# w_o with the samples' two parts in one stationary block, and VectorE's residual taken in halves

## The chip, the core and the metric

The kernel runs on one core of a Trainium2 chip. A time is the device time of one execution in microseconds (us); beside it the hardware profiler gives a trace of one execution, with its span. The engines are TensorE (PE in the rows; PEld is its loading of stationary weights), VectorE (DVE), ScalarE (ACT), GpSimd (POOL) and SyncE (SP), which issues most of the transfers. Each works through a queue of its own in order and waits for the others on semaphores.

## What is computed

One layer of a decoder trunk, for 512 rows of a prompt and 8 rows of samples that share the weights. After the mixer's branches are merged into m, the output projection w_o, a gated residual, a second norm and the router follow, and then the experts that the router chose:

```python
def _mixer(h, buf_a, buf_b, buf_c, pos0, w_in, conf_dw, conf_dw_b, conf_ln_g, conf_ln_b,
           conf_pw, pool_w, pool_scale, sc_dw, sc_out, w_o):
    ...
    m = jax.nn.sigmoid(z_ga) * y_a + jax.nn.sigmoid(z_gb) * y_b + jax.nn.sigmoid(z_gc) * y_c
    return jnp.einsum('btd,de->bte', m, w_o), nb_a, nb_b, nb_c

def _moe(h, rg, rg_b, re, re_b, w1, w3, w2):
    ...
    gp = jax.nn.softmax((hf @ rg + rg_b).astype(jnp.float32), axis=-1)
    gidx = jnp.argmax(gp, axis=-1)
    ...
    el = (hf @ re + re_b).astype(jnp.float32).reshape(-1, N_GROUPS, EXP_PER_GROUP)
    ...
    for e in range(N_EXPERTS):
        act = jax.nn.silu(hf @ w1[e]) * (hf @ w3[e])
        y = y + (act @ w2[e]) * comb[:, e:e + 1]
    return y.reshape(b, t, d)

def _run_group(x, c, st_a, st_b, st_c, pos0, P):
    ...
        sh1, s1, g1, sh2, s2, g2 = jnp.split(mod[:, None, :], 6, axis=-1)
        h = _rmsnorm(x, P['norm1_g'][l]) * (1 + s1) + sh1
        m, na, nb, nc = _mixer(h, ...)
        x = x + g1 * m
        h = _rmsnorm(x, P['norm2_g'][l]) * (1 + s2) + sh2
        x = x + g2 * _moe(h, P['router_g'][l], P['router_g_b'][l], P['router_e'][l], ...)
    y = _rmsnorm(x, P['final_g'])
```

D_MODEL is 1024, there are 4 groups of 4 experts with 512 hidden columns each.

## The kernel before

The 520 rows are five row tiles: four of 128 prompt rows, and tile 4 with the 8 samples. All large products keep float32 accuracy by splitting both operands into two parts (hi and lo, type fp32r) and adding three products: hi x hi, hi x lo, lo x hi (`three`, L652 to L659). Weights arrive by SP's queue in quarters of 128x1024 into a ring of 6 raw slots; ScalarE makes the hi part of a quarter (`hi`, L1148), VectorE the lo part (`lo`, L1592), into rings of 4 slots; TensorE's semaphore quarter_used frees a slot. The order on each engine is written out by hand.

The stage of this change runs from 417 to 506 us of the trace:

- w_o has 1024 output columns, taken as two passes of 512. Its stationary operand is a block of the merged rows (hT_hi, hT_lo: 128 channels x the rows of a tile), its moving operand 512 columns of w_o. The first pass (L897 to L907) goes through the 8 blocks of channels, and in each through the five tiles, three matmuls each, into PSUM banks 0 to 4. The second pass (`w_o_tile`) goes tile by tile, 24 matmuls each, into banks 5 and 6 in turn; tile i waits for t_ready i-1, so that VectorE has read tile i-2's bank.
- Behind each tile VectorE does `residual` (x1 += gate x result: two multiplies of 512 columns and one add of 1024), `row_means`, and for the tile before it `second_norm`: four tiny operations for the reciprocal root, then h2 = x1 x r x scale and h2 += shift, 1024 columns each.
- ScalarE squares and sums each tile of x1 (`squares_of`), copies the transposed h2 of tile i-2 out of PSUM (`turned_h2`), issues the store of h2 of tile i-1 (`store_h2`) and takes the root (`root_of`), in this order for i = 0 to 6; at i = 5 it first splits two quarters of expert weights (`his(0, 2)`).
- TensorE puts between the tiles of the second pass the transposes of h2 (`router_turn`) and the router's logits (`router_logits`), and fills in "gap products": 16 products of 512 columns (L953) for a gate that is needed only at the end, 2, 2, 4, 1, 6 and 1 of them in six places. Their weights are loaded by `gap_load` on SP's queue; gap_prepared says that their 16-column stationary operand c_pad and the scales are ready.

```python
            for i in range(NTILE + 2):
                if i < NTILE:
                    w_o_tile(i)
                ...
                if i >= 3:
                    router_logits(i - 3)
                if i >= 2:
                    router_turn(i - 2)
            router_logits(NTILE - 1)
```

From the last logits VectorE works out each row's experts (L1982 to L2000), TensorE counts them, and the first 128 rows for the experts are gathered; the experts' loop runs on to the end.

## Time and profile before

| | |
|---|---|
| median of 3 runs | 871.22 us (870.71 to 872.97) |
| the profiled execution | 873.34 us, its span 871.5 us |
| TensorE busy | 837.3 us, 96% of the span |
| VectorE busy | 686.0 us, 79% |
| ScalarE busy | 465.5 us, 53% |
| GpSimd busy | 77.0 us, 9% |

The span is what the trace covers; 1.84 us of the execution lie around it. A row of a timeline gives the start, the duration, engine and line, what is written and read, and in brackets how long the engine was idle before and what ended that. A matmul's duration covers its way through the pipeline, so the distance from start to start is what one costs in a stream. An fp32 matmul stands as two entries.

### The profile page before, as it was taken

What the parts mean: (1) busy time and instruction counts of PE and PEld (TensorE: products, weight loads), DVE (VectorE), ACT (ScalarE), POOL (GpSimd) and SP (SyncE); (2) the same over time, 40 slices, a digit from 0 to 9 for tenths busy, and PEclk for the clock granted to TensorE, in tenths of its full rate; (3) what the DMA queues carried; (4) which work ended last, traced back from release to release, by engine and by line L of the source; (5) the groups of instructions that cost most, each with busy time, mean ns of one, the idle gap of its engine ahead of it and who ended that gap; (6) DMA issues with size and microseconds to landing.
All of it is one profiled execution on the core that took longest, in us unless ns stands there. A gap on an engine that the chain in (4) does not pass through costs nothing.

```text
span 871.5 us, 14885 instructions
## 1 busy us (share of the span) xinstructions
PE 837.3 (96%) x5035; PEld 699.3 (80%) x5035; DVE 686.0 (79%) x942; ACT 465.5 (53%) x556; POOL 77.0 (9%) x71
## 2 busy tenths in 40 slices
PE   7899999999999999999999889999999999999994
PEld 2589999989899999899777457888888888887851
DVE  0681638878798679599438879999989999899888
ACT  4552442343422221642222457888888888888852
POOL 0002000000000000230000001000100001003750
PEclk9889999999999999999999999999999999999998
DMA  9858545445443321123671579988896899999962
GB/s 329 276 166 277 200 126 170 138 151 164 148 152 118 97 80 66 55 74 123 237 251 73 175 275 390 393 313 317 312 400 219 322 398 400 400 399 397 359 196 98
DMA packets 90997, 201.24 MB, mean 231 GB/s; under 512 B 8792, under 2 KB 13400, under 8 KB 90918
## 3 DMA queue, kind: packets, MB, share of 16 engines
q1 hardware_dynamic: 78813, 165.25, 53.8%
q0 software_dynamic: 5136, 18.42, 6.0%
q10 hardware_dynamic: 7003, 16.95, 5.2%
q8 instruction: 30, 0.49, 0.2%
q14 instruction: 15, 0.12, 0.0%
HBM read 182.97 MB, written 18.35 MB: 231 GB/s over the span
## 4 chain that ended last, share of the span: by engine, by line
PE 81%; DVE 9%; DMA 3%; ACT 2%; issue 2%; SPq 1%; ACTq 1%; POOL 0%; POOLq 0%; DVEq 0%
PE ps L806 31%; PE ps L657 12%; PE ps L659 12%; PE ps L658 12%; PE ps L886 3%; DVE w_lo L1592 2%; PE ps L1001 2%; DMA region_a<-in_x_prompt_dram 2%; PE ps L1123 1%; PE ps L685 1%; PE ps L686 1%; PE ps L838 1%; ACT w_hi L1148 1%; DMA region_b<-h_rows,slot_idx 1%; PE ps L1036 1%
## 5 line engine op out<-in xcount | busy, mean ns | idle before, releaser
L1592 DVE TENSOR_TENSOR w_lo<-raw,w_hi 128x1024 fp32r<-128x1024 f32 x202 | 241.5, 1225 | 100.1 <-ACT w_hi L1148 98.3
L1148 ACT ACTIVATE w_hi<-raw 128x1024 fp32r<-128x1024 f32 x202 | 207.9, 1056 | 198.2 <-PE ps L806 150.6
L657 PE MATMUL ps<-w_hi,hT_hi 128*128 128x512 f32 (+1 forms) x512 | 205.6, 401 | 3.6 <-DVE w_lo L1592 1.4
L659 PE MATMUL ps<-w_hi,hT_lo 128*128 128x512 f32 (+1 forms) x512 | 202.1, 395 | 0.0
L658 PE MATMUL ps<-w_lo,hT_hi 128*128 128x512 f32 (+1 forms) x512 | 201.5, 393 | 0.0
L806 PE MATMUL ps<-hT_hi,w_hi 128*128 128x260 f32 x768 | 156.4, 285 | 1.9 <-ACT region_b L1242 1.1
L806 PE MATMUL ps<-hT_lo,w_hi 128*128 128x260 f32 x768 | 155.0, 283 | 0.0
L806 PE MATMUL ps<-hT_hi,w_lo 128*128 128x260 f32 x768 | 154.9, 283 | 0.0
L806 PEld LDWEIGHTS ps<-hT_hi,w_hi 128*128 128x128 f32 x768 | 118.8, 189 | 5.2 <-DVE w_lo L1592 3.9
L806 PEld LDWEIGHTS ps<-hT_lo,w_hi 128*128 128x128 f32 x768 | 119.4, 190 | 0.0
L806 PEld LDWEIGHTS ps<-hT_hi,w_lo 128*128 128x128 f32 x768 | 118.9, 189 | 0.0
L657 PEld LDWEIGHTS ps<-w_hi,hT_hi 128*128 128x128 f32 (+1 forms) x512 | 94.6, 185 | 28.8 <-DVE w_lo L1592 3.1
L1592 DVE TENSOR_TENSOR w_lo<-region_a,w_hi 128x1024 fp32r<-128x1024 f32 x90 | 110.3, 1244 | 6.2 <-ACT w_hi L1148 5.6
L659 PEld LDWEIGHTS ps<-w_hi,hT_lo 128*128 128x128 f32 (+1 forms) x512 | 94.5, 184 | 24.2
L658 PEld LDWEIGHTS ps<-w_lo,hT_hi 128*128 128x128 f32 (+1 forms) x512 | 94.7, 185 | 22.5
L1148 ACT ACTIVATE w_hi<-region_a 128x1024 fp32r<-128x1024 f32 x90 | 95.2, 1062 | 28.1 <-PE ps L659 28.1
L1739 DVE SCALAR_TENSOR_TENSOR region_b<-region_b,pT 128x512 f32<-128x512 f32 x120 | 81.7, 735 | 0.0
L1518 POOL DMA_INDIRECT region_b<-h_rows,slot_idx x18 | 23.0, 1280 | 381.0 <-DVE slot_idx L1969 271.4
L1592 DVE TENSOR_TENSOR hT_lo<-ps,hT_hi 128x512 fp32r<-128x512 f32 (+1 forms) x37 | 34.4, 933 | 13.0 <-ACT hT_hi L1401 10.4
L1497 POOL TENSOR_TENSOR hT_lo<-region_b,hT_hi 128x520 fp32r<-128x520 f32 x8 | 12.0, 1531 | 297.1 <-ACT hT_hi L1263 275.6
L1255 ACT ACTIVATE region_a<-ps 128x520 f32<-128x520 f32 x24 | 14.6, 606 | 33.7 <-PE ps L806 33.7
L685 PE MATMUL ps<-w_hi,cT 128*48 128x512 f32 x64 | 27.1, 423 | 2.0 <-DVE w_lo L1592 1.7
(337 smaller groups left out, 838.6 us busy)
## 6 DMA issues: line engine op xcount, KB each, us to landing
raw<-in_exp_w_dram SPq DMA_DIRECT2D x96, 512.0 KB
region_a<-in_exp_w_dram SPq DMA_DIRECT2D x80, 512.0 KB
raw<-in_w_in_dram SPq DMA_DIRECT2D x48, 512.0 KB
raw<-in_w_ada_dram SPq DMA_DIRECT2D x30, 512.0 KB
expert_rows<-region_b ACTq DMA_DIRECT2D x17, 512.0 KB, 6.3
region_b<-in_exp_w_dram SPq DMA_DIRECT2D x16, 512.0 KB
region_b<-in_w_ada_dram SPq DMA_DIRECT2D x14, 512.0 KB, 8.1
expert_rows<-region_a POOLq DMA_DIRECT2D x8, 512.0 KB, 8.4
```

The source lines that it names most:

```text
L657: pe.matmul(out, pairs[0], moving[0], start=start, stop=False)
L658: pe.matmul(out, pairs[0], moving[1], start=False, stop=False)
L659: return pe.matmul(out, pairs[1], moving[0], start=False, stop=stop)
L685: pe.matmul(ps[0:C_LO + 16, bank, :], cT[:, kk, :], hi[:, k, :], start=(kk == 0), stop=False)
L806: mm = pe.matmul(ps[:, 2 * m + h, 0:HT], w[:, k, ms], x[:, kk, h * HT:(h + 1) * HT], start=start, stop=stop)
L886: mm = pe.matmul(ps[:, 2 * s + h, 0:HT], w[:, k, (t % 2) * P:(t % 2 + 1) * P], x[:, kk, h * HT:(h + 1) * HT], start=start, stop=stop)
L1001: t = pe.transpose(ps[:, 2 + k // 4, (k % 4) * P:(k % 4 + 1) * P], xg[:, k * P:(k + 1) * P], ident[:, :])
L1148: act.activation(w_hi[:, split_slot(n), :], place, ACT.Copy).then_inc(hi_done, 1)
L1255: act.activation(split(gates[:, 4 * (g - 6) + m, :]), halves(m), ACT.Sigmoid).then_inc(set_free[m], 1)
L1518: pool.indirect_dma_start(xg, None, h2_dram, bass.IndirectOffsetOnAxis(ap=slot_idx[:, :], axis=0)).then_inc(xg_ready, 16)
L1592: return dve.tensor_tensor(out, whole, first.bitcast(F32), ALU.subtract)
L1739: dve.scalar_tensor_tensor(va[:, c, 0:NP], ua[:, c, t:t + NP], w, va[:, c, 0:NP], ALU.mult, ALU.add).then_inc(conv_step, 1)
```

## The change

- A tile cT of 48 columns for each of the 8 channel blocks exists before (it holds the conditioning for the adaLN products, hi part in columns 0 to 15 and lo part from column C_LO = 32). When those products are over, VectorE forms c_pad from it early (gap_prepared 1), and GpSimd copies the samples' hi and lo parts of the merged rows into columns 0 to 7 and 32 to 39, block by block behind VectorE's lo part (sampled_ready).
- w_o's tile 4 then takes this block of 40 columns as stationary operand, with two matmuls (w_o's hi, w_o's lo) in place of three; the two parts' results stand in PSUM rows 0 to 7 and 32 to 39 and are added by VectorE.
- VectorE's residual is cut into a left half (columns 0 to 511, out of the first pass' banks) and a right half. The left halves of tiles 0 and 1 stand behind the first pass, those of 2, 3 and 4 between the steps of tiles 0 and 1. `second_norm` of a tile now follows in the tile's own turn; the scale is multiplied in ahead of the root (`scaled`), and the root and the shift go in one operation.
- The scaling of SC2 moves ahead of the last two lo parts of w_o; SP's fourth gap_load waits for gap_prepared 2, which comes with it. The gap products stand 1, 1, 5, 1, 6 and 2 in the six places.

ScalarE's and SP's order is the same as before. The first place is VectorE ahead of w_o's second pass. Before, all four lo parts (L1592, the first of them stands above the piece), the scales, c_pad, and the first tile's residual:

```order
L1592 TENSOR_TENSOR w_lo<-raw,w_hi 128x1024 [waits hi_done] x3
L1895 SCALAR_TENSOR_TENSOR region_a<-region_a 128x1024 [waits ld_dec,ld_bcast]
L1896 SCALAR_TENSOR_TENSOR region_a<-region_a 8x1024 [waits dve_step]
L1897 TENSOR_TENSOR small<-cT 128x128 [waits gap_prepared]
L1930 TENSOR_TENSOR region_b<-ps,region_a 128x512 [waits ld_router,wo_done,ld_x,gap_prepared]
```

The same place in the changed kernel, with its own line numbers (L1609 is the lo part, L1953 and L1954 are a left half, L1969 and L1970 a right half, L1979 is `scaled`):

```order
L1609 TENSOR_TENSOR w_lo<-raw,w_hi 128x1024 [waits hi_done,dve_step]
L1609 TENSOR_TENSOR w_lo<-raw,w_hi 128x1024 [waits hi_done]
L1913 SCALAR_TENSOR_TENSOR region_a<-region_a 128x1024 [waits ld_dec,ld_bcast]
L1914 SCALAR_TENSOR_TENSOR region_a<-region_a 8x1024 [waits dve_step]
L1609 TENSOR_TENSOR w_lo<-raw,w_hi 128x1024 [waits hi_done,gap_prepared]
L1609 TENSOR_TENSOR w_lo<-raw,w_hi 128x1024 [waits hi_done]
L1953 TENSOR_TENSOR region_b<-ps,region_a 128x512 [waits quarter_used,ld_router,ld_x]
L1954 TENSOR_TENSOR region_a<-region_a,region_b 128x512 [waits dve_step]
L1953 TENSOR_TENSOR region_b<-ps,region_a 128x512 [waits dve_step]
L1954 TENSOR_TENSOR region_a<-region_a,region_b 128x512 [waits dve_step]
L1969 TENSOR_TENSOR region_b<-ps,region_a 128x512 [waits wo_done,dve_step]
```

The scales moved ahead of two lo parts, c_pad is gone from here, and two left halves stand ahead of the first wait for w_o's second pass.

The second place is VectorE around the samples' residual. Before, from the residual of tile 3 on (L1914 to L1918 are the root of tile 2, L1942 and L1944 its h2, L1908 and L1924 the mean of tile 3 and a logit tile):

```order
L1930 TENSOR_TENSOR region_b<-ps,region_a 128x512 [waits wo_done,ms_ready]
L1931 TENSOR_TENSOR region_b<-ps,region_a 128x512
L1932 TENSOR_TENSOR region_a<-region_a,region_b 128x1024 [waits t_ready]
L1914 RECIPROCAL sums<-sums 128x1 [waits root_ready,x1_ready]
L1916 SCALAR_TENSOR_TENSOR sums<-sums 128x1 [waits dve_step]
L1917 TENSOR_SCALAR sums<-sums 128x1 [waits dve_step]
L1918 TENSOR_TENSOR sums<-sums 128x1 [waits dve_step]
L1942 SCALAR_TENSOR_TENSOR region_b<-region_a,sums 128x1024 [waits dve_step]
L1944 TENSOR_TENSOR region_b<-region_b,region_a 128x1024 [waits dve_step]
L1908 TENSOR_SCALAR sums<-sums 128x1 [waits ssq_ready]
L1924 TENSOR_TENSOR region_b<-ps,rbias 128x20 [waits logit_done,ms_ready]
L1930 TENSOR_TENSOR region_b<-ps,region_b 8x512 [waits quarter_used]
```

After, the same stretch; L1933 to L1937 are now the root of tile 3 itself, L1985 its h2:

```order
L1969 TENSOR_TENSOR region_b<-ps,region_a 128x512 [waits wo_done]
L1970 TENSOR_TENSOR region_a<-region_a,region_b 128x512 [waits t_ready]
L1979 TENSOR_TENSOR region_b<-region_a 128x1024 [waits h2_stored0,h2T_done,x1_ready]
L1927 TENSOR_SCALAR sums<-sums 128x1 [waits ssq_ready,dve_step]
L1943 TENSOR_TENSOR region_b<-ps,rbias 128x20 [waits logit_done,ms_ready]
L1933 RECIPROCAL sums<-sums 128x1 [waits root_ready]
L1935 SCALAR_TENSOR_TENSOR sums<-sums 128x1 [waits dve_step]
L1936 TENSOR_SCALAR sums<-sums 128x1 [waits dve_step]
L1937 TENSOR_TENSOR sums<-sums 128x1 [waits dve_step]
L1985 SCALAR_TENSOR_TENSOR region_b<-region_b,sums,region_a 128x1024 [waits dve_step]
L1967 TENSOR_TENSOR region_b<-ps,region_b 8x512 [waits quarter_used]
```

The root that stands between two residuals is that of the tile just done (tile 3), where it was that of the tile before (tile 2).

The third place is TensorE behind w_o's last tile (the samples), where a row "x7" is the rest of 8 matmuls. Before:

```order
L939 MATMUL ps<-wrouter,region_b 128x20 [waits h2T_ready]
L939 MATMUL ps<-wrouter,region_b 128x20 x7
L932 MATMUL ps<-ident,region_b 128x128 [waits h2T_ready,h2_ready]
L932 MATMUL ps<-ident,region_b 128x128 x7
L953 MATMUL ps<-region_b,small 16x512 [waits nat_ready0,gap_prepared,t_ready]
L953 MATMUL ps<-region_b,small 16x512
```

After (L950 logits, L943 transposes, L964 gap products):

```order
L904 MATMUL ps<-w_lo,cT 40x512
L950 MATMUL ps<-wrouter,region_b 128x20 [waits h2T_ready]
L950 MATMUL ps<-wrouter,region_b 128x20 x7
L943 MATMUL ps<-ident,region_b 128x128 [waits h2T_ready,h2_ready]
L943 MATMUL ps<-ident,region_b 128x128 x7
L964 MATMUL ps<-region_b,small 16x512 [waits nat_ready0,gap_prepared,t_ready]
L950 MATMUL ps<-wrouter,region_b 128x20 [waits h2T_ready]
```

One gap product stands where two stood, ahead of the logits of tile 2; it is the same ahead of those of tile 3.

```diff
--- before.py
+++ after.py
...
@@ -615,7 +616,7 @@
             for h in range(3):
                 gap_load(h)
             up_weights(0, exp_w1, 0, None)
-            sp.wait_ge(gap_prepared, 1)
+            sp.wait_ge(gap_prepared, 2)
             gap_load(3)
             up_weights(4, exp_w3, 0, None)
             sp.wait_ge(h2_ready, NTILE)
@@ -887,10 +888,20 @@
                 mm.then_inc(unit_done(12 + t)[0], 1)
+            def w_o_rows(i):
+                return P if i < NTILE - 1 else C_LO + ND
             def w_o_part(out, i, q, k, w):
                 n = rows(i)
                 hi, lo = w
                 kk = MERGE_ORDER[2 * q + k]
+                if i == NTILE - 1:
+                    pe.wait_ge(sampled_ready, 2 * q + k + 1)
+                    x = cT[:, kk, 0:C_LO + ND]
+                    pe.matmul(out, x, hi[:, k, :], start=(q == 0 and k == 0), stop=False)
+                    return pe.matmul(out, x, lo[:, k, :], start=False, stop=(q == 3 and k == 1))
                 x = (hT_hi[:, kk, i * P:i * P + n], hT_lo[:, kk, i * P:i * P + n])
                 return three(out, x, (hi[:, k, :], lo[:, k, :]), q == 0 and k == 0, q == 3 and k == 1)
...
@@ -962,15 +973,15 @@
                     pe.wait_ge(t_ready, NTILE - 1)
                     pe.wait_ge(gap_prepared, 2)
-                    gap_products(2)
+                    gap_products(1)
                 elif i == NTILE + 1:
-                    gap_products(2)
+                    gap_products(1)
                 if i >= 3:
                     router_logits(i - 3)
                 if i >= 2:
                     router_turn(i - 2)
             router_logits(NTILE - 1)
-            gap_products(4)
+            gap_products(5)
             pe.wait_ge(onehot_ready, 1)
@@ -1043,7 +1054,7 @@
                 if kk == 3:
                     t.then_inc(first_half_turned, 1)
             t.then_inc(xgT_done, 1)
-            gap_products(1)
+            gap_products(2)
             pe.wait_ge(first_half_lo, 1)
             first = (first_hi, first_lo)
             up(0, 0, 0, first, range(1))
@@ -1506,6 +1517,12 @@
             branch_rest(KW, sbr, sbr_hi_done, sbr_lo_done)
             branch_rest(0, va, va_hi_done, va_lo_done)
+            pool.wait_ge(gap_prepared, 1)
+            for p, j in enumerate(MERGE_ORDER):
+                pool.wait_ge(m_lo_done, p + 1)
+                pool.tensor_copy(cT[:, j, 0:ND], hT_hi[:, j, NP:NT])
+                pool.tensor_copy(cT[:, j, C_LO:C_LO + ND], hT_lo[:, j, NP:NT]).then_inc(sampled_ready, 1)
             for p in range(3):
                 pool.wait_ge(h2_stored[p], 16 * ((NTILE + 2 - p) // 3))
@@ -1818,6 +1835,7 @@
                     short_conv(q - 44)
             dve.wait_ge(conv_ready, 1)
+            link(dve.tensor_tensor(c_pad, cT[:, :, 0:16].bitcast(F32), cT[:, :, C_LO:C_LO + 16].bitcast(F32), ALU.add), gap_prepared, 1)
             dve.tensor_tensor(tmp_b[:, 0:NT], va[:, 0, :], va[:, 1, :], ALU.add).then_inc(pair_summed, 1)
             dve.tensor_tensor(tmp_a[:, 0:NT], va[:, 2, :], va[:, 3, :], ALU.add).then_inc(pair_summed, 1)
             dve.wait_ge(pair_summed, 2)
@@ -1887,14 +1905,15 @@
             for pad in (tiles16, scan_a, scan_b):
                 dve.memset(pad[:, 0:8], 0.0)
             link(dve.memset(logits[:, :, :], 0.0))
-            for q in range(4, 8):
+            for q in (4, 5):
                 lo(N_WO + q)
             dve.wait_ge(ld_bcast, 16 * 5)
             dve.wait_ge(ld_dec, 16 * 3)
             link(dve.scalar_tensor_tensor(bvec[:, SC2, :], bvec[:, SC2, :], 1.0, n2b, ALU.add, ALU.mult))
-            link(dve.scalar_tensor_tensor(sc2_dec[0:ND, :], sc2_dec[0:ND, :], 1.0, n2b[0:ND, :], ALU.add, ALU.mult), gap_prepared, 1)
-            link(dve.tensor_tensor(c_pad, cT[:, :, 0:16].bitcast(F32), cT[:, :, C_LO:C_LO + 16].bitcast(F32), ALU.add), gap_prepared, 2)
+            link(dve.scalar_tensor_tensor(sc2_dec[0:ND, :], sc2_dec[0:ND, :], 1.0, n2b[0:ND, :], ALU.add, ALU.mult), gap_prepared, 2)
+            for q in (6, 7):
+                lo(N_WO + q)
             dve.wait_ge(ld_x, 16 * NTILE)
             dve.wait_ge(ld_router, 64)
@@ -1923,36 +1942,65 @@
                 dve.wait_ge(logit_done, i + 1)
                 dve.tensor_tensor(logits[0:n, i, :], ps[0:n, i, 0:NR], rbias[0:n, :], ALU.add).then_inc(logits_ready, 1)
-            def residual(i):
+            def gate1(i):
+                return bvec[:, G1, :] if i < NP // P else g1_dec[0:ND, :]
+            def residual_left(i):
+                n = rows(i)
+                part = t_row[0:n, 0:COLS]
+                link(dve.tensor_tensor(part, ps[0:n, i, :], gate1(i)[:, 0:COLS], ALU.mult))
+                link(dve.tensor_tensor(x1[0:n, i, 0:COLS], x1[0:n, i, 0:COLS], part, ALU.add))
+                if i == NTILE - 1:
+                    link(dve.tensor_tensor(part, ps[C_LO:C_LO + n, i, :], gate1(i)[:, 0:COLS], ALU.mult))
+                    link(dve.tensor_tensor(x1[0:n, i, 0:COLS], x1[0:n, i, 0:COLS], part, ALU.add))
+            def residual_right(i):
                 n = rows(i)
                 dve.wait_ge(*((wo_done, i + 1) if i < NTILE - 1 else (quarter_used, splits(N_WO + 7))))
-                g1 = bvec[0:n, G1, :] if i < NP // P else g1_dec[0:ND, :]
-                dve.tensor_tensor(t_row[0:n, 0:COLS], ps[0:n, i, :], g1[:, 0:COLS], ALU.mult)
-                link(dve.tensor_tensor(t_row[0:n, COLS:D], ps[0:n, 5 + i % 2, :], g1[:, COLS:D], ALU.mult), t_ready, i + 1)
-                link(dve.tensor_tensor(x1[0:n, i, :], x1[0:n, i, :], t_row[0:n, :], ALU.add), x1_ready, i + 1)
+                part = t_row[0:n, COLS:D]
+                if i == NTILE - 1:
+                    link(dve.tensor_tensor(part, ps[C_LO:C_LO + n, 5 + i % 2, :], gate1(i)[:, COLS:D], ALU.mult))
+                    link(dve.tensor_tensor(x1[0:n, i, COLS:D], x1[0:n, i, COLS:D], part, ALU.add))
+                link(dve.tensor_tensor(part, ps[0:n, 5 + i % 2, :], gate1(i)[:, COLS:D], ALU.mult), t_ready, i + 1)
+                link(dve.tensor_tensor(x1[0:n, i, COLS:D], x1[0:n, i, COLS:D], part, ALU.add), x1_ready, i + 1)
+            def scaled(i):
+                n = rows(i)
+                if i >= 3:
+                    dve.wait_ge(h2T_done, i - 2)
+                    dve.wait_ge(h2_stored[i % 3], 16 * (i // 3))
+                sc2 = bvec[0:n, SC2, :] if i < NP // P else sc2_dec[0:ND, :]
+                link(dve.tensor_tensor(h2[i % 3][0:n, :], x1[0:n, i, :], sc2, ALU.mult))
             def second_norm(i):
                 n = rows(i)
                 r = row_rsqrt(i, i, 3 + i)
-                if i >= 3:
-                    dve.wait_ge(h2T_done, i - 2)
-                    dve.wait_ge(h2_stored[i % 3], 16 * (i // 3))
-                sc2 = bvec[0:n, SC2, :] if i < NP // P else sc2_dec[0:ND, :]
-                link(dve.scalar_tensor_tensor(h2[i % 3][0:n, :], x1[0:n, i, :], r, sc2, ALU.mult, ALU.mult))
                 shift = bvec[0:n, SH2, :] if i < NP // P else sh2_dec[0:ND, :]
-                dve.tensor_tensor(h2[i % 3][0:n, :], h2[i % 3][0:n, :], shift, ALU.add).then_inc(h2_ready, 1)
-            for i in range(NTILE + 1):
-                if i < NTILE:
-                    residual(i)
-                if i:
-                    second_norm(i - 1)
-                if i < NTILE:
-                    row_means(i, i, NTILE + i + 1, 3 + i)
+                dve.scalar_tensor_tensor(h2[i % 3][0:n, :], h2[i % 3][0:n, :], r, shift, ALU.mult, ALU.add).then_inc(h2_ready, 1)
+            dve.wait_ge(quarter_used, splits(N_WO + 3))
+            residual_left(0)
+            residual_left(1)
+            for i in range(NTILE):
+                residual_right(i)
+                scaled(i)
+                if i == 0:
+                    residual_left(2)
+                row_means(i, i, NTILE + i + 1, 3 + i)
+                if i == 0:
+                    residual_left(3)
+                elif i == 1:
+                    residual_left(4)
                 if i >= 3:
                     logit_tile(i - 3)
+                second_norm(i)
+            logit_tile(NTILE - 3)
             dve.memset(fresh_flags[:, 0, 0:1], 1)
             dve.memset(fresh_flags[:, 1, 0:2], 1)
             dve.tensor_copy(tile_f, tile_no[:, 0:MAX_TILES])
```

## Rows read from the trace of the kernel before

**Rows 1.** Timeline of TensorE: w_o's start, and two of the samples' matmuls.
```profile
417.36 0.47 PE L657 MATMUL ps<-w_hi,hT_hi 128*128 128x512 f32 x1 [0.88 <-DVE tmp_b L1863]
...
423.72 0.40 PE L657 MATMUL ps<-w_hi,hT_hi 128*8 128x512 f32 x1
...
424.19 0.40 PE L659 MATMUL ps<-w_hi,hT_lo 128*8 128x512 f32 x1
```
**Rows 2.** Timeline of TensorE from the logits of tile 0 to the counting.
```profile
469.19 1.86 PE L939 MATMUL ps<-wrouter,region_b 128*128 128x20 f32 x16
470.89 1.07 PE L932 MATMUL ps<-ident,region_b 128*128 128x128 f32 x8
...
480.04 1.89 PE L953 MATMUL ps<-region_b,small 128*16 128x512 f32 x4
482.25 1.96 PE L939 MATMUL ps<-wrouter,region_b 128*128 128x20 f32 x16 [0.32 <-ACT region_b L1352]
...
490.33 1.88 PE L953 MATMUL ps<-region_b,small 128*16 128x512 f32 x4
492.04 1.88 PE L953 MATMUL ps<-region_a,small 128*16 128x512 f32 x4
495.22 0.18 PE L981 MATMUL ps<-onehot_both,before 128*128 128x16 bf16 x1 [1.30 <-DVE onehot_both L2000]
```
**Rows 3.** Timeline of VectorE: tile 1's residual, tile 0's norm, the samples, the last logits.
```profile
457.30 0.68 DVE L1931 TENSOR_TENSOR region_b<-ps,region_a 128x512 f32<-128x512 f32 x1
458.02 1.22 DVE L1932 TENSOR_TENSOR region_a<-region_a,region_b 128x1024 f32<-128x1024 f32 x1
459.27 0.16 DVE L1914 RECIPROCAL sums<-sums 128x1 f32<-128x1 f32 x1
...
460.11 1.28 DVE L1942 SCALAR_TENSOR_TENSOR region_b<-region_a,sums 128x1024 f32<-128x1024 f32 x1
...
477.54 0.68 DVE L1930 TENSOR_TENSOR region_b<-ps,region_b 8x512 f32<-8x512 f32 x1 [1.84 <-PE ps L659]
...
490.52 0.17 DVE L1924 TENSOR_TENSOR region_b<-ps,rbias 8x20 f32<-8x20 f32 x1 [0.20 <-PE ps L939]
```
**Rows 4.** Timeline of ScalarE: tile 2's squares to its root, then ahead of tile 3's copies.
```profile
465.33 1.06 ACT L1331 ACTIVATE region_b<-region_a 128x1024 f32<-128x1024 f32 x1 [2.06 <-DVE region_a L1932]
...
466.39 1.07 ACT L1352 ACTIVATE region_b<-ps 128x512 f32<-128x512 f32 x2
468.75 0.33 ACTq L1342 DMA_DIRECT2D h_rows<-region_b  x1
469.13 0.20 ACT L1336 ACTIVATE sums<-sums 128x1 f32<-128x1 f32 x1 [1.67 <-DVE sums L1908]
...
483.99 1.99 ACT L1148 ACTIVATE w_hi<-raw 128x1024 fp32r<-128x1024 f32 x2
485.88 1.06 ACT L1352 ACTIVATE region_b<-ps 128x512 f32<-128x512 f32 x2
```
**Rows 5.** Stretches of 2 us: length; PE, PEld, DVE, ACT, POOL busy; PEclk; DMA.
```profile
36.00:38.00 2.00, 1.13 (x4) 0.41 (x4) 1.97 (x5) 1.64 (x2) 0.00 (x0) 0.90 0.80 239
38.00:40.00 2.00, 1.65 (x4) 0.63 (x4) 2.00 (x3) 0.00 (x0) 0.00 (x0) 0.50 0.78 230
...
50.00:52.00 2.00, 2.00 (x14) 2.00 (x13) 1.97 (x4) 0.00 (x0) 0.00 (x0) 0.69 0.49 164
```
**Rows 6.** Timeline of TensorE in and behind that stretch.
```profile
38.35 0.66 PE L685 MATMUL ps<-w_hi,cT 128*48 128x512 f32 x1 [1.11 <-DVE w_lo L1592]
...
41.17 1.87 PE L748 MATMUL ps<-fold,region_b 48*128 48x9 f32 x8
...
52.21 1.05 PE L748 MATMUL ps<-fold,region_b 48*128 48x9 f32 x8
```
**Rows 7.** Timelines of GpSimd and VectorE where both read SBUF at once.
```profile
382.22 3.29 POOL L1497 TENSOR_TENSOR hT_lo<-region_b,hT_hi 128x520 fp32r<-128x520 f32 x2 [21.26 <-ACT hT_hi L1293]
...
384.26 2.33 DVE L1592 TENSOR_TENSOR w_lo<-raw,w_hi 128x1024 fp32r<-128x1024 f32 x1
```

9 lines of the change are left out of this document (5 added, 4 removed).

## Prediction

> **What bounds the stage now.** I read the timelines of TensorE, VectorE and ScalarE between 417 and 520 us side by side, because the change touches nothing else, and asked at each wait who comes last. The point that sets everything behind is the last logit: VectorE takes it at 490.52 [rows 3], works without a break to the experts' one-hot rows, TensorE counts them at 495.22 after 1.30 us idle [rows 2], and from there the chain goes on to the gathers. So a gain or loss of the change is the shift of 490.52, unless TensorE is late at 495.22.
>
> Up to the samples' tile TensorE is the bound. It streams through w_o, and VectorE waits 1.84 us for the samples' result at 477.54 [rows 3]. Behind that a chain through three engines takes over: samples' residual, squares, copies of h2T of tile 2, and only then the logits of tile 2 at 482.25, for which TensorE waits 0.32 us although it had two gap products to do [rows 2]. The copies for tile 3 start at 485.88, late because ScalarE first makes two hi parts from 483.99 [rows 4].
>
> **TensorE's work.** A samples' matmul costs (424.19 - 423.72) / 2 = 0.235 us from start to start [rows 1]. Eight go in each pass: -1.9 us in the first, which PE would end 1.9 us earlier, and -1.9 us in tile 4. The matmul with 40 stationary columns has 512 moving columns as before; those with 48 columns of the same tile show no different cost. Two gap products go from between the logits to behind them; one costs (492.04 - 490.33) / 2 = 0.86 us [rows 2]. Together TensorE has 3.8 + 1.7 = 5.5 us less to do before the last logit. That is the most that can be gained.
>
> **VectorE's work.** A linked operation of 512 columns costs 458.02 - 457.30 = 0.72 us, one of 1024 columns 459.27 - 458.02 = 1.25, the root's four 460.11 - 459.27 = 0.84, the last operation of 1024 columns about 1.20 where the next does not wait for it (1.28 long, [rows 3]), the mean 0.18. A prompt tile costs now two halves of 1.44, 1.25 scaled, 0.18, 0.84, 1.20: 6.35 us, against 6.05 before. The samples cost 2 x 2.88 for their halves, since each has two multiplies and two adds.
> The first pass starts at 417.36 [rows 1] and with 112 matmuls for 120 ends at 443.5. ScalarE's last hi part and VectorE's last lo part take until 445.8; the left halves of tiles 0 and 1 take 2.9 more, to 448.7, hidden behind w_o's tile 0, which ends at 449.1. So 2.9 us of VectorE's work are really taken out of its chain.
> From 449.3 VectorE never waits: tile 0 costs 1.44 + 1.25 + 1.44 + 0.18 + 1.44 + 0.84 + 1.20 = 7.8 us (with the left halves of 2 and 3), tile 1 1.44 + 1.25 + 0.28 + 2.88 + 0.84 + 1.20 = 7.9 (with the samples' left half). The right half of tile 2 starts at 465.0, while w_o's tile 2 was done at 460.3. VectorE is the bound here, where before it was TensorE.
>
> **The lock step.** The root of a tile is now needed before the next tile's residual. In ScalarE's order it stands behind the squares, the copies of h2T of the tile two before and a store: 1.06 + 1.05 + 0.37 + 0.20 us [rows 4]. So from one right half to the next: 1.44 + 1.06 + 1.05 + 0.37 + 0.20 + 0.84 + 1.20 = 6.2 us with the hand-overs, of which VectorE idles 1.3. Before, the root had a whole residual as its cover. Tile 3's right half is at 471.2, the samples' at 477.4. Before it was 477.54. The 1.9 + 1.9 us of TensorE and the 2.9 of VectorE have gone into this step.
> From there: the samples' half 2.88 to 480.3 (before 2.6), squares and copies to 482.4, logits of tile 2 at 482.5, 0.2 us later than before; logits and transposes 1.81 + 0.95, so tile 3 is transposed at 485.4. Here something is won: ScalarE's root of the samples comes at 483.0 instead of 483.9, its two hi parts are over by 485.0, and the copies start at once at 485.4 instead of 485.88. The last logit comes at 490.0, **0.5 us earlier**.
> Five products of 0.86 then end at 494.3, ahead of the one-hot rows at 494.7. The second product behind the first gathered rows costs between 0 and its own 0.86 us; the wait for VectorE's lo part and the later wait for the second gather cover most of it, and I book 0.1. Sum without anything else: **-0.4 us**.
>
> **What hides the rest.** c_pad's 0.3 us move to the end of the mixer's branches, where TensorE still works on w_in long after VectorE's sum is ready. The scales move into VectorE's wait for ScalarE behind w_o's second lo part, so the two lo parts behind them aren't late; SP's fourth gate load and two expert loads go some 5 to 14 us earlier, into transfers that are over before anything of this stage waits for one. GpSimd's 16 copies of 8 columns have no row like them. The nearest above is a 128x520 operation, 3.29 / 2 = 1.65 us [rows 7]; at 3.3 us a block the copies keep up with TensorE's 3.3 us a block, from which they have 3 us of lead in the first block and more than 10 in the fifth. I book 0, between 0 and 1.
> While GpSimd ran, VectorE's lo part took 2.33 us instead of 1.22 [rows 7]. So copies of 8 columns may hold VectorE a little between 402 and 412 us, where it catches up with TensorE and waits for it. The Trainium skill (SBUF — State Buffer, section on the two separate sides) says that the two engines share a port pair which one holds for a whole instruction; the trace agrees.
>
> **The rival that I take for the likeliest: the clock falls.** After the samples' tile TensorE has too little left. Its tile 3 ends at 466.8 and the logits of tile 0 wait for copies until 468.5 (1.7 us idle); tile 4 ends at 474.9, logits and transposes at 477.6, one product at 478.5, and then there is nothing until 482.5: **4.0 us idle**, and behind it only logits and transposes, which are short matmuls. Before, two products stood there and the idle time was 0.3.
> In this kernel the granted clock fell once in the middle of work: at 37.6 us (0.90 over the stretch 36 to 38, 0.50 behind it [rows 5]), after transposes of a few columns and waits of 0.6 and 1.1 us [rows 6]. That is the lower level, 1.2 in place of 2.4 GHz, and it was granted back at 51.2 (0.69 over 50 to 52), 13.6 us later, though TensorE was mostly busy. The wait of 1.30 us ahead of 495.22 [rows 2] did not lower it, with products on both sides. A wait of 4.0 us among short matmuls is worse than what lowered it.
> Price by rows: the same 8 entries of L748 took 1.87 us at the lower level and 1.05 at the upper [rows 6], a factor 1.78. Logits of tile 2 +1.45, transposes of tile 3 +0.8, the product now longer than ScalarE's copies +0.6, logits of tile 3 +1.5, transposes and logits of the samples +0.7: +5.0 if all of it is hit. The five products then cost up to 1.72 each in place of 0.86, and TensorE comes late for the counting by another 1.5 (if the clock is back after two or three of them) to 4. Least: only the logits of tile 2 are hit, -0.4 + 1.4 = +1.0. Most by a length like that of the trace: -0.4 + 5.0 + 1.6 = +6.2. Nothing in the rows fixes the moment; I take the middle, **+3.6 us: 874.8**.
> The Trainium skill (TensorE: Matmul & The Clock Gate, on HAM oscillation) tells the same of waits between groups of matmuls: the array falls back to half rate and must earn the full rate again. Its half rate would double a stream and not take 1.78 of it; by it the most would be about 1 us more.
>
> **The other rivals.**
> 1. No fall. The schedule above stands alone: 870.8, between 869.8 and 871.7. For it speaks that the 1.30 us ahead of 495.22 did nothing; against it the 4.0 us.
> 2. TensorE stays the bound, because VectorE and ScalarE are quicker than the lock step says. Then up to 5.5 us come out: 865.8, half of it 868.5. It needs VectorE's tile at some 4.9 us instead of 6.2. The durations speak against it; the same adding up of the rows of before gives its own 490.52 to 0.1 us.
> 3. The samples' copies hold up tile 4 in the first pass: it decides from 5.4 us for a pair of copies in the last four blocks; a pair of 7 would cost 6 us more. The 1.65 of a far larger operation speaks against it.
>
> **How the numbers follow.** Clock falls: 0.70. No fall: 0.19. TensorE-bound gain: 0.07. Others, slower: 0.04. The sum is made on one execution of 873.34 us (span 871.5); the median is 2.1 lower, and as the stage has no state of its own I put the shift on the median: 871.22 + 3.6 = 874.8. The range goes from the no-fall case (870.8 less 1.0) to 6.2 + 0.8 above the median: 869.8 to 878.2. Within 0.3% (2.6 us, about what a measurement of this kernel can tell from no change) lie the no-fall case and some 0.3 of the falls; slower are 0.7 of the falls and the others: faster 0.08, same 0.39, slower 0.53.
>
> **What would show it.** Right: TensorE idle for about 4 us ahead of the logits of tile 2, near 482.5; VectorE without a wait from the first right half to that of tile 2, then 1.1 to 1.4 us ahead of each root; the granted clock below 1 in the stretches between 480 and 496; logits of tile 3 at over 3 us. Wrong: logits of tile 2 before 481, or a clock of 1.00 throughout with the last logit at 490.0. If the samples' matmuls of the first pass show waits on GpSimd, rival 3 holds. The forecast is most easily wrong in when the clock falls and how soon it is given back.

## The result, and the profile after the change

| | before | after |
|---|---|---|
| median | 871.70 us (20 runs, 868.69 to 873.83) | 874.75 us (20 runs, 871.13 to 877.19) |
| ratio, 95% interval | | 1.0034 (1.0022 to 1.0046) |
| the profiled execution | 873.34 us, span 871.5 | 872.93 us, span 871.2 |
| mean granted clock there | 0.988 | 0.984 |

The change makes the kernel 0.34% slower, some 3 us. The forecast was 874.8 us. The profiled execution of after is one of the quicker ones, that of before (873.34 us) one of before's slower ones: after's is the shorter by 0.4 us. So its rows show where the clock falls and what that costs there, but not the loss of 3 us; that rests on the 20 runs of each.

TensorE in the timeline of after, behind w_o's tile 3 (L950 logits, L943 transposes, L903 and L904 the samples in tile 4, L964 gap products, L992 the counting), to be laid beside [rows 2]:

```profile
468.64 1.96 PE L950 MATMUL ps<-wrouter,region_b 128*128 128x20 f32 x16 [1.93 <-ACT region_b L1363]
470.44 1.07 PE L943 MATMUL ps<-ident,region_b 128*128 128x128 f32 x8
471.27 0.67 PE L903 MATMUL ps<-w_hi,cT 128*40 128x512 f32 x1
471.74 0.63 PE L904 MATMUL ps<-w_lo,cT 128*40 128x512 f32 x1
...
474.30 0.63 PE L904 MATMUL ps<-w_lo,cT 128*40 128x512 f32 x1
474.73 0.44 PE L903 MATMUL ps<-w_hi,cT 128*40 128x512 f32 x1
475.00 0.39 PE L904 MATMUL ps<-w_lo,cT 128*40 128x512 f32 x1
...
476.38 0.40 PE L904 MATMUL ps<-w_lo,cT 128*40 128x512 f32 x1
...
481.82 1.96 PE L950 MATMUL ps<-wrouter,region_b 128*128 128x20 f32 x16 [1.48 <-ACT region_b L1363]
...
489.33 4.84 PE L964 MATMUL ps<-region_b,small 128*16 128x512 f32 x8
494.01 1.02 PE L964 MATMUL ps<-region_a,small 128*16 128x512 f32 x2
494.96 0.18 PE L992 MATMUL ps<-onehot_both,before 128*128 128x16 bf16 x1
```

The samples' matmuls stand (474.30 - 471.74) / 6 = 0.43 us apart in the first half of tile 4 and (476.38 - 475.00) / 6 = 0.23 in the second. The five gap products ahead of the counting take from 489.33 to 494.96, 1.13 us each for 0.86. The clock shows why, in stretches of 2 us of after (length; PE, PEld, DVE, ACT, POOL busy; PEclk; DMA):

```profile
470.00:472.00 2.00, 2.00 (x16) 1.68 (x16) 1.97 (x3) 0.00 (x0) 0.00 (x0) 0.85 0.03 8
472.00:474.00 2.00, 2.00 (x6) 0.86 (x5) 1.78 (x4) 1.75 (x4) 0.00 (x0) 0.50 0.40 162
474.00:476.00 2.00, 2.00 (x9) 0.93 (x8) 1.36 (x5) 0.47 (x2) 0.00 (x0) 0.80 0.27 104
...
488.00:490.00 2.00, 1.63 (x24) 0.98 (x24) 0.45 (x4) 1.54 (x4) 0.00 (x0) 0.61 0.03 8
490.00:492.00 2.00, 2.00 (x4) 0.41 (x3) 1.71 (x9) 1.92 (x2) 0.00 (x0) 0.53 0.55 136
```

It is at the lower level (0.50, 1.2 GHz) twice: about 471.4 to 474.8, behind the wait of 1.93 us and the short matmuls of the logits and transposes, and about 488.4 to 491.9, from just ahead of the samples' logits at 488.80 on. In before's trace it is 1.00 throughout this stage, here for one stretch:

```profile
472.00:474.00 2.00, 2.00 (x10) 0.79 (x9) 1.83 (x6) 1.96 (x4) 0.00 (x0) 1.00 0.00 0
```

VectorE in after, the answer to [rows 3]:

```profile
465.01 0.69 DVE L1969 TENSOR_TENSOR region_b<-ps,region_a 128x512 f32<-128x512 f32 x1
...
468.78 0.16 DVE L1933 RECIPROCAL sums<-sums 128x1 f32<-128x1 f32 x1 [0.90 <-ACT sums L1347]
...
470.81 0.68 DVE L1969 TENSOR_TENSOR region_b<-ps,region_a 128x512 f32<-128x512 f32 x1
...
474.50 0.16 DVE L1933 RECIPROCAL sums<-sums 128x1 f32<-128x1 f32 x1 [0.62 <-ACT sums L1347]
...
476.81 0.68 DVE L1967 TENSOR_TENSOR region_b<-ps,region_b 8x512 f32<-8x512 f32 x1 [0.20 <-PE ps L904]
...
489.54 0.17 DVE L1943 TENSOR_TENSOR region_b<-ps,rbias 8x20 f32<-8x20 f32 x1 [1.49 <-PE ps L950]
493.93 0.24 DVE L2048 TENSOR_TENSOR onehot_both<-region_b 128x80 bf16<-128x80 f32 x1
```

The last logit comes at 489.54, 0.98 us ahead of before's 490.52. The one-hot rows are ready at 494.17, but TensorE counts only at 494.96, for before's 495.22: most of what was won is gone by then.

### The profile page after: what moved, and what is told of

It is laid out like the page before. It is cut to its first block, busy times and chain, and to the rows that moved or that the text cites. A ratio compares the mean times of both kernels' runs of the same rounds, so it can differ in the third digit from the quotient of the medians.

```text
span 871.2 us, 14883 instructions
## 1 busy us (share of the span) xinstructions
PE 836.7 (96%) x5019; PEld 699.7 (80%) x5019; DVE 690.1 (79%) x951; ACT 465.3 (53%) x556; POOL 81.5 (9%) x87
## 3 DMA queue, kind: packets, MB, share of 16 engines
q10 hardware_dynamic: 7003, 16.95, 5.3%
## 4 chain that ended last, share of the span: by engine, by line
PE 81%; DVE 8%; DMA 4%; ACT 3%; issue 2%; ACTq 1%; SPq 1%; POOL 0%; POOLq 0%; DVEq 0%
PE ps L807 31%; PE ps L658 11%; PE ps L660 11%; PE ps L659 11%; PE ps L887 3%; DVE w_lo L1609 2%; PE ps L1012 2%; DMA region_a<-in_x_prompt_dram 2%; DMA region_b<-h_rows,slot_idx 1%; PE ps L1134 1%; PE ps L686 1%; PE ps L687 1%; PE ps L839 1%; ACT w_hi L1159 1%; PE ps L964 1%
## 5 line engine op out<-in xcount | busy, mean ns | idle before, releaser
L1609 DVE TENSOR_TENSOR w_lo<-raw,w_hi 128x1024 fp32r<-128x1024 f32 x202 | 241.5, 1225 | 94.7 <-ACT w_hi L1159 92.9
L658 PE MATMUL ps<-w_hi,hT_hi 128*128 128x512 f32 x496 | 199.2, 402 | 3.3 <-DVE w_lo L1609 1.4
L660 PE MATMUL ps<-w_hi,hT_lo 128*128 128x512 f32 x496 | 195.8, 395 | 0.0
L659 PE MATMUL ps<-w_lo,hT_hi 128*128 128x512 f32 x496 | 195.2, 394 | 0.0
L1609 DVE TENSOR_TENSOR w_lo<-region_a,w_hi 128x1024 fp32r<-128x1024 f32 x90 | 110.3, 1243 | 6.4 <-ACT w_hi L1159 5.8
L658 PEld LDWEIGHTS ps<-w_hi,hT_hi 128*128 128x128 f32 x496 | 93.2, 188 | 27.0 <-DVE w_lo L1609 3.1
L660 PEld LDWEIGHTS ps<-w_hi,hT_lo 128*128 128x128 f32 x496 | 93.0, 188 | 21.9
L659 PEld LDWEIGHTS ps<-w_lo,hT_hi 128*128 128x128 f32 x496 | 93.3, 188 | 20.3
L1609 DVE TENSOR_TENSOR hT_lo<-ps,hT_hi 128x512 fp32r<-128x512 f32 (+1 forms) x37 | 34.4, 932 | 12.8 <-ACT hT_hi L1412 10.4
```

Source lines behind the costliest of these rows:

```text
L658: pe.matmul(out, pairs[0], moving[0], start=start, stop=False)
L659: pe.matmul(out, pairs[0], moving[1], start=False, stop=False)
L660: return pe.matmul(out, pairs[1], moving[0], start=False, stop=stop)
L1609: return dve.tensor_tensor(out, whole, first.bitcast(F32), ALU.subtract)
```

## The measure for the experiments

The start of w_o differs between executions (414.33 to 417.64 us in the traces below), so I compare stretches: A from w_o's first matmul to the start of the samples' last residual half (in before their whole residual), B from there to the last logit. "Clock" is the median over a kernel's runs of the mean granted clock. The ratio is to before on the same chip in the same runs; its median and clock were 871.84 us and 0.989 beside e1 to e4, 871.61 and 0.987 beside e5 to e8, 869.75 and 0.991 beside e9 to e11, 869.94 and 0.991 beside e12. So kernels of different groups are to be compared by their ratios, not by their microseconds.

| kernel | median us | ratio (95%) | clock | A | B | A + B |
|---|---|---|---|---|---|---|
| before | 871.70 | 1 | 0.987 to 0.991 | 60.18 | 12.98 | 73.16 |
| after | 874.75 | 1.0034 (1.0022, 1.0046) | 0.9815 | 59.43 | 12.73 | 72.16 |
| e1 gap products as before | 874.05 | 1.0018 (0.9998, 1.0037) | 0.9825 | 61.09 | 14.94 | 76.03 |
| e2 transposes, partly misplaced | 874.38 | 1.0028 (1.0010, 1.0046) | 0.9855 | 59.29 | 16.50 | 75.79 |
| e3 norm behind | 871.57 | 1.0003 (0.9987, 1.0020) | 0.985 | 55.72 | 16.95 | 72.67 |
| e4 samples' passes alone | 873.85 | 1.0024 (1.0009, 1.0039) | 0.983 | 59.23 | 16.57 | 75.80 |
| e5 VectorE's order alone | 871.09 | 0.9999 (0.9983, 1.0014) | 0.987 | 60.06 | 12.50 | 72.56 |
| e6 after, waits filled | 872.65 | 1.0013 (0.9990, 1.0035) | 0.987 | 59.28 | 12.65 | 71.93 |
| e7 norm behind, filled | 868.99 | 0.9969 (0.9952, 0.9987) | 0.986 | 55.78 | 12.93 | 68.71 |
| e8 gap products late | 879.87 | 1.0101 (1.0076, 1.0127) | 0.976 | 59.27 | 17.30 | 76.57 |
| e9 norm behind, 2 products | 867.09 | 0.9968 (0.9949, 0.9987) | 0.990 | 55.73 | 12.94 | 68.67 |
| e10 e4, waits filled | 870.18 | 1.0003 (0.9990, 1.0017) | 0.987 | 59.23 | 13.46 | 72.69 |
| e11 e7, 4 and 7 products | 866.50 | 0.9949 (0.9932, 0.9966) | 0.990 | 55.75 | 13.07 | 68.82 |
| e12 e8, waits filled | 875.28 | 1.0053 (1.0038, 1.0069) | 0.984 | 59.42 | 13.29 | 72.71 |

B is the telling column: 12.5 to 13.5 us where the clock stays up from the first mark until about the last logits, and 14.9 to 17.3 where it falls well ahead of them.

## Experiments: the clock

**e1: useful work back in the waits.**

```diff
@@ after: the six places of gap_products
-1, 1, 5, 1, 6, 2
+2, 2, 4, 1, 6, 1
```


> The changed kernel with the gap products as before: 2, 2, 4, 1, 6 and 1 in the six places instead of 1, 1, 5, 1, 6 and 2. It gives back 0.86 us of work to each of TensorE's idle places ahead of the logits of tile 2 (1.48 us in the trace of after) and of tile 3 (0.21 us). Theory (the clock falls because TensorE runs out of work between tile 4 and the last logits): the fall at about 488.4 us is gone, the one at 471.4, ahead of which no product stands, stays; the logits of tile 3 and the last logits come about 1 us earlier at full clock, less 0.65 us because the second product is now in the way of the logits of tile 3: 873.5 us, clock 1.00 between 476 and 496. Rival (the schedule alone is the loss, the falls come whatever stands there): 0.65 us later at the last logit, 875.4 us, the clock below 1 behind 485 as before.

Ratio 1.0018, and the second fall is not gone. In the profiled execution the clock fell three times between 466 and 496, first about 468.6, at the start of the logits of tile 0 (3.61 us for 1.96). Neither theory as I wrote it fits: two products more didn't hold the clock in that execution, and the interval doesn't separate this kernel from after.

**e2: unread transposes, partly in the wrong place.**

```diff
@@ after: ahead of router_logits(i - 3)
+                if i == 3:
...
+                    keep_running(12)
...
+                elif i == NTILE + 1:
+                    keep_running(9)
```


> The changed kernel with work that nobody reads in TensorE's two idle places: 12 transposes of the identity (128x128, into a free bank, about 0.12 us each) ahead of the logits of tile 0, and 9 ahead of those of tile 2. They are meant to end before ScalarE's copies come (1.93 and 1.48 us idle in the trace of after). Theory (idle time between short matmuls lowers the clock): both falls, at 471.4 and 488.4 us, are gone, the granted clock is 1.00 in every stretch between 466 and 496; the 8 samples' matmuls at 0.43 us cost 0.23 again (-1.6 us), the gap products and the logits behind 488.4 about -1.5: 871.0 to 872.5 us. Rival (the falls do not hang on these waits): 874.75 us within 0.6, clock as in after.

The second group was put one place too late: with i == NTILE + 1 it stands ahead of the logits of tile 3. So this run filled only the first wait; the nine transposes, from 486.66 us on, held up the logits of tile 3 to 488.41 instead, though ScalarE's copies for them were ready at 486.03. Behind the first wait the clock stayed at 1.00 until past 480, the samples' matmuls cost 0.23 us, and the wait ahead of the logits of tile 2 grew to 2.89 us; the clock fell at about 481.3, in the logits behind it. In TensorE's timeline of e2:

```profile
480.38 2.75 PE L950 MATMUL ps<-wrouter,region_b 128*128 128x20 f32 x16 [2.89 <-ACT region_b L1376]
482.96 1.95 PE L943 MATMUL ps<-ident,region_b 128*128 128x128 f32 x8
```

This is close to the picture that the prediction drew (a wait of 4.0 us there). After's profiled execution is a different one: there the earlier fall had made tile 4 longer and the wait shorter.

**e6: one-pass matmuls in all the places.** Data that is there anyway, into a free PSUM bank (the conditions and two waits for t_ready are left out here):

```diff
+            def keep_running(count, bank):
+                for _ in range(count):
+                    pe.matmul(ps[:, bank, :], hT_hi[:, 0, 0:P], hT_hi[:, 0, 0:COLS], start=True, stop=True)
@@ ahead of the logits of tile 0, 2, 3 and of the samples
+                    keep_running(6, 4)
+                    keep_running(8, 4)
+                    keep_running(1, 4)
+            keep_running(1, 5)
```


> The changed kernel with work that nobody reads in TensorE's idle places, this time one-pass matmuls of 512 moving columns (0.23 us each) and in the places meant: 6 ahead of the logits of tile 0, 8 ahead of those of tile 2, 1 ahead of those of tile 3 and 1 ahead of the samples'. Theory (the waits lower the clock, and the clock is the loss): the mean granted clock over the runs is 0.987 or more, as high as before's, against 0.982, and the time follows it by the slope of the runs of after (0.001 of clock for 0.47 us): -2.4 us, 872.4 us, at full clock between 466 and 496 in the profiled run. The lock step stays, so the time stays above before's 871.7. Rival (clock and waits have nothing to do with each other, both follow the time of the run): clock 0.982 as after, 874.75 us plus the delays of the added matmuls, up to 1 us.

Measured 872.65 us, clock 0.987: both as the clock theory said. In the profiled execution A + B is 71.93 us, 1.2 less than before's. But the ratio's interval overlaps that of after, so this run alone is no proof. In the timeline and the stretches of e6:

```profile
478.83 2.11 PE L972 MATMUL ps<-hT_hi 128*128 128x512 f32 x8
481.76 1.96 PE L950 MATMUL ps<-wrouter,region_b 128*128 128x20 f32 x16 [0.82 <-ACT region_b L1378]
```
```profile
472.00:474.00 2.00, 2.00 (x10) 0.96 (x9) 1.88 (x4) 1.64 (x4) 0.00 (x0) 1.00 0.36 145
...
490.00:492.00 2.00, 2.00 (x4) 0.44 (x3) 1.70 (x9) 1.87 (x2) 0.00 (x0) 0.50 0.55 189
```

The logits of tile 2 start at 481.76 although 1.9 us of idle time were filled, so the filling delays nothing. Around the last logits the clock fell here too.

**e8: the dose.** The waits made longer by taking two useful products out of them.

```diff
@@ after: the six places of gap_products
-1, 1, 5, 1, 6, 2
+0, 0, 6, 1, 7, 2
```


> The changed kernel with still less for TensorE to do between its waits: gap products 0, 0, 6, 1, 7 and 2 in the six places. The wait ahead of the logits of tile 2 grows by 0.86 us, that ahead of the logits of tile 3 too. Theory (waits lower the clock): the mean granted clock is below the 0.982 of the changed kernel, and the time is 1 us longer or more: 875.8 us. Rival (schedule alone): nothing waits for these two products, the logits of tile 3 are held up 0.0 us less, 874.75 us within 0.6 or up to 0.3 less.

879.87 us, ratio 1.0101, clock 0.976. The direction is the clock theory's, the size is 5 times what it forecast, and the rival (no loss from moving them) is out: 5 us are lost. How much of that is the clock and how much the products' later place, e12 shows. Timeline and stretches of e8:

```profile
481.20 3.57 PE L950 MATMUL ps<-wrouter,region_b 128*128 128x20 f32 x16 [3.94 <-ACT region_b L1363]
...
487.73 3.60 PE L950 MATMUL ps<-wrouter,region_b 128*128 128x20 f32 x16 [1.17 <-ACT region_b L1363]
```
```profile
476.00:478.00 2.00, 1.26 (x12) 1.02 (x11) 1.90 (x4) 0.00 (x0) 0.00 (x0) 0.98 0.00 0
478.00:480.00 2.00, 0.00 (x0) 0.00 (x0) 1.93 (x3) 1.05 (x2) 0.00 (x0) 0.50 0.71 190
...
496.00:500.00 4.00, 4.00 (x7) 0.74 (x6) 1.98 (x12) 0.32 (x2) 0.00 (x0) 0.70 0.92 309
```

The clock is down for 20 us at a stretch, from about 477.9, early in the wait of 3.94 us, to about 498.4. The two groups of logits cost 3.6 us each.

**e12: e8 with the waits filled** (6, 13, 4 and 1 of the unread matmuls).

> The kernel with the gap products late (0, 0, 6, 1, 7, 2), whose median was 1.0101 of before's with a median clock of 0.976, and unread matmuls of 512 columns (0.23 us each) in its waits: 6 ahead of the logits of tile 0, 13 ahead of those of tile 2, 4 ahead of those of tile 3, 1 ahead of the samples'. No useful work is moved. Theory (TensorE's waits lower the clock, and that alone is the loss there): the median clock goes up to 0.986 or more, the stretch from w_o's first matmul to the last logit from 76.6 to 72 us, the time to 1.000 to 1.003 of before's. Rival (the products were missed for their results or their place, not for the work): 1.010 again, and the unread matmuls add up to 0.5 us.

Ratio 1.0053 for 1.0101, with intervals that don't touch: work that nobody reads, put into the waits, takes back about 4 us (half of the loss). This is the cleanest evidence here that the waits cost through the clock. The median clock came to 0.984 and not 0.986, and the time missed its forecast by some 2 us. Two things show in the trace. The six products ahead of the counting end at 496.1, though the one-hot rows are ready at 494.64, and the transposes of the gathered rows start at 504.54 with no wait for the gather, which before waited 0.54: the late products are themselves on the path, which my rival to e8 had denied. And the clock fell at about 471.5 all the same:

```profile
468.53 1.96 PE L950 MATMUL ps<-wrouter,region_b 128*128 128x20 f32 x16 [0.53 <-ACT region_b L1378]
470.34 1.07 PE L943 MATMUL ps<-ident,region_b 128*128 128x128 f32 x8
...
496.10 0.18 PE L1007 MATMUL ps<-onehot_both,before 128*128 128x16 bf16 x1
```
```profile
472.00:474.00 2.00, 2.00 (x6) 0.82 (x5) 1.68 (x4) 1.84 (x4) 0.00 (x0) 0.50 0.46 188
```

In e6 the same place, with 0.55 us left of the wait, kept 1.00; up to there the two kernels have the same order. So with the same order and nearly the same wait the clock falls in one execution and not in another.

## Experiments: the parts, and the lock step

**e4: the samples' two passes alone**, VectorE's order as before (only the samples' left half ahead of their right half).

```diff
@@ VectorE
-            for i in range(NTILE):
-                residual_right(i)
-                scaled(i)
+            for i in range(NTILE + 1):
+                if i < NTILE - 1:
+                    residual(i)
+                elif i == NTILE - 1:
+                    residual_left(i)
+                    residual_right(i)
+                if i:
+                    whole_norm(i - 1)
...
```


> The TensorE part of the change alone: the samples' two passes for three, with GpSimd's copies; VectorE's residuals and norms and the gap products (2, 2, 4, 1, 6, 1) as before the change, only the samples' left half (2.88 us) in front of their right half, in VectorE's wait for TensorE. By adding up: TensorE ends the samples' tile at 473.7 instead of 477.5, VectorE has finished tile 3 at 473.8 and the left half at 476.7, the right half at 479.6 against 480.1 us before. Theory (lock step and clock are both the loss): -0.5 us against before, 871.2 us, if the clock stays up, and 872.8 us if it falls behind the logits of tile 0 as in after. Rival (the samples' tile in two passes is itself slower than it looks, by the copies on GpSimd or by the doubled adds): 874 us or more, with waits in the first pass.

873.85 us (two of its runs, at 1030 and 1180 us, count neither here nor in the ratio), ratio 1.0024 (1.0009 to 1.0039): the part that relieves TensorE makes the kernel slower by itself. The time lies between what theory (872.8) and rival (874 or more) gave it, but the rival's sign is missing: TensorE's rows of the first pass show no wait for GpSimd. A is 0.95 us shorter than before's, and B 3.6 us longer, with a wait of 3.37 us and the clock at 0.50 behind it:

```profile
480.06 3.09 PE L950 MATMUL ps<-wrouter,region_b 128*128 128x20 f32 x16 [3.37 <-ACT region_b L1363]
```

**e10: e4 with the waits filled** (11, 1 and 1).

> The samples' two passes alone (which took 873.85 us without its two disturbed runs, 2 us over before) with 11 unread matmuls of 512 columns in the wait of 3.37 us ahead of the logits of tile 2, and 1 each ahead of the logits of tile 3 and of the samples. Theory (the two passes alone lose only through the clock: TensorE ends early and waits): the stretch from w_o's first matmul to the last logit is 72.5 us at full clock instead of 75.8, the time 871 us, that of before within 0.8. Rival (the doubled adds and GpSimd's copies lose it): 873.85 us within 0.7.

Ratio 1.0003 (0.9990 to 1.0017), no longer different from before; A + B is 72.69 us for 75.80, forecast 72.5. The stretch from 476 to 486 us ran at 1.00. The doubled adds and GpSimd's copies are all still there, so they are not what e4's trace lost; the clock behind TensorE's early end is. By time alone it is not quite shown, since the two intervals overlap a little. In e10's timeline:

```profile
476.82 2.83 PE L972 MATMUL ps<-hT_hi 128*128 128x512 f32 x11
480.26 1.96 PE L950 MATMUL ps<-wrouter,region_b 128*128 128x20 f32 x16 [0.60 <-ACT region_b L1379]
```

**e5: VectorE's order alone**, three passes for the samples, gap products as before the change.

```diff
@@ w_o_part
-                if i == NTILE - 1:
-                    pe.wait_ge(sampled_ready, 2 * q + k + 1)
-                    x = cT[:, kk, 0:C_LO + ND]
...
@@ residual_left, residual_right
-                if i == NTILE - 1:
-                    link(dve.tensor_tensor(part, ps[C_LO:C_LO + n, i, :], ...
```


> The VectorE part of the change alone: left halves ahead and between, norm in the tile's own turn, scales and c_pad moved as in the change; the samples' tile in three passes, no copies on GpSimd, gap products 2, 2, 4, 1, 6, 1 as before. Theory (VectorE's new order makes a lock step that loses what the halves win): in the trace of the run with the norm behind, the stretch from the first to the last right half took 3.7 us less than in the changed kernel; with TensorE's 3.8 us back in the sum this kernel is slower than before: 874 to 876 us. Rival (the two passes are what loses): 871.8 us within 0.6, and the change minus this one would be the loss.

Ratio 0.9999 (0.9983 to 1.0014): my theory fell. The lock step wins nothing but loses nothing either, since TensorE with its full work is late for the samples anyway (VectorE waits 0.47 us for it). Here the clock stayed at 1.00 from 460 until past 486.

**e3: the lock step opened.** In after, the norm of a tile goes behind the next right half.

```diff
@@ VectorE
-            for i in range(NTILE):
-                residual_right(i)
-                scaled(i)
+            for i in range(NTILE + 1):
+                if i < NTILE:
+                    residual_right(i)
+                if i:
+                    second_norm(i - 1)
+                if i < NTILE:
+                    scaled(i)
...
-                second_norm(i)
```


> The changed kernel with the norm of a tile behind the right half of the next tile, as before the change, so that the root has a residual as its cover; halves, the samples' two passes and the gap products as in the changed kernel. Theory of the prediction (the lock step of right half, squares, root, norm eats the gain): VectorE's waits of 0.90, 0.62 and 0.62 us ahead of the roots go, the samples' right half starts when TensorE has ended tile 4, and the last logit comes up to 1.5 us earlier: 873.3 us. Rival (in the trace of after the samples' right half waited for TensorE, 0.20 us, so the lock step no longer binds; the clock is the loss): nothing to gain, 874.75 us within 0.6, and a clock below 1 between 466 and 496 as in after.

871.57 us. A fell from 59.3 to 55.7 us: the lock step did bind, by 3.6 us, more than twice what I expected of it, and the rival ("it no longer binds") had read the wait of 0.20 us for TensorE too literally: that one existed because the clock had slowed tile 4. But B took 16.95 us, so that most of it went again. Timelines of TensorE, then VectorE (the right halves of tiles 2 and 3, and the samples'), of e3:

```profile
475.99 2.75 PE L950 MATMUL ps<-wrouter,region_b 128*128 128x20 f32 x16 [1.47 <-ACT region_b L1363]
...
482.26 3.60 PE L950 MATMUL ps<-wrouter,region_b 128*128 128x20 f32 x16
```
```profile
460.74 0.69 DVE L1969 TENSOR_TENSOR region_b<-ps,region_a 128x512 f32<-128x512 f32 x1
...
465.67 0.69 DVE L1969 TENSOR_TENSOR region_b<-ps,region_a 128x512 f32<-128x512 f32 x1
...
470.98 0.68 DVE L1967 TENSOR_TENSOR region_b<-ps,region_b 8x512 f32<-8x512 f32 x1 [0.20 <-PE ps L904]
```

**e9 and e7: both losses taken away.** e9 is e3 with the gap products at 2, 1, 5, 1, 6, 1; e7 has 2, 1 and 1 unread matmuls ahead of the logits of tiles 2, 3 and of the samples besides.

> The kernel with the norm behind the next right half, and its TensorE kept at work: 2 gap products ahead of the logits of tile 2 and 1 ahead of those of tile 3, with 2, 1 and 1 unread matmuls of 512 columns (0.23 us each) ahead of the logits of tiles 2, 3 and of the samples. In the trace of the kernel with the norm behind, the clock was 0.50 from about 477 to 491 us, behind a wait of 1.47 us, and the stretch from the samples' right half to the last logit took 16.95 us against 12.73 in the changed kernel. Theory (lock step and clock are two separate losses): with both gone the stretch is 12.5 us at full clock, the time 867.5 to 869 us, faster than before and after. Rival (what the lock step gives back can't be kept, the clock falls with any order that has less work for TensorE): the clock falls here too, 871.5 us within 1.

> The kernel with the norm behind the next right half and the gap products at 2, 1, 5, 1, 6, 1; nothing unread. One product more than in the kernel with the norm behind, in the wait of 1.47 us ahead of the logits of tile 2. Theory (the length of the wait among short matmuls matters): 0.6 us of wait is left there, the clock falls less often than in the kernel with the norm behind (0.985) and more often than in the one with the unread matmuls too (0.986 to 0.993 in most runs): 869 to 871 us. Rival (only a TensorE without any wait keeps the clock): 871.5 us as with the norm behind.

Ratios 0.9969 and 0.9968. B is 12.9 us in both. One useful product in the wait of 1.47 us does as well as that product and the unread matmuls together: 0.62 us of wait is left in e9, and the clock is up until past 484. The rival of e9 is out. Its theory isn't confirmed in all either: I had the clock fall more often in e9 than in e7, but each lies 0.001 below the before beside it. In e9's timeline:

```profile
477.22 1.96 PE L950 MATMUL ps<-wrouter,region_b 128*128 128x20 f32 x16 [0.62 <-ACT region_b L1363]
```

**e11: the fastest.** e7 with the gap products at 2, 1, 4, 1, 7, 1.

> The fastest kernel so far (norm behind, gap products 2, 1, 5, 1, 6, 1, unread matmuls 2, 1, 1) with the gap products at 2, 1, 4, 1, 7, 1: one product leaves the place between the last logits and the counting, where the clock had fallen to 0.50 and TensorE came 1.2 us later than VectorE's one-hot rows. Theory (at half clock five products are on the path): where the clock falls there the counting comes 0.9 us earlier, the seventh product behind it costs 0.3: 868.4 us, 0.6 less than 868.99. Rival (the products behind the counting are on the path as much): 869.0 within 0.5.

Ratio 0.9949 (0.9932 to 0.9966), 866.5 us: it beats before by 0.5% and after by some 0.8%. The forecast of 868.4 us started from e7's 868.99, beside which before took 871.61; here it took 869.75, so the 866.5 say less than the ratio. Against e7 and e9 the intervals overlap, so the gain of the moved product is likely, not shown. The marks fit it: TensorE counts at 491.19, 0.08 us behind the one-hot rows, where in e7 it was 1.26 late. From w_o's first matmul to the transposes of the first gathered rows it is 81.99 us in e11, 82.79 in e9 and 86.05 in before. The clock still falls around the last logits, about 485.7 to 489.1 (timeline of VectorE, then stretches, of e11):

```profile
473.39 0.68 DVE L1982 TENSOR_TENSOR region_b<-ps,region_b 8x512 f32<-8x512 f32 x1 [0.24 <-PE ps L904]
...
486.46 0.17 DVE L1958 TENSOR_TENSOR region_b<-ps,rbias 8x20 f32<-8x20 f32 x1 [1.48 <-PE ps L950]
```
```profile
474.00:484.00 10.00, 9.87 (x62) 6.47 (x61) 9.46 (x26) 5.15 (x9) 0.00 (x0) 1.00 0.34 109
...
486.00:488.00 2.00, 2.00 (x16) 0.58 (x13) 1.30 (x7) 1.98 (x3) 0.00 (x0) 0.50 0.15 23
```

## Why the prediction was right, and where its steps were off

- **TensorE's work, the first pass, the halves: right.** The first pass ended at 443.4 (forecast 443.5), the left halves at 448.8 (448.7), tile 0's right half began at 449.26, tile 1's 7.85 us later (7.8), tile 2's at 465.01 (465.0). A matmul with 40 stationary columns costs 0.23 us like the others.
- **Which part loses.** The samples' two passes alone give 1.0024 (e4), VectorE's order alone 0.9999 (e5), both with the gap products as before 1.0018 (e1), the whole change 1.0034. So the loss comes with the work taken from TensorE; what the two moved gap products add to it the intervals don't separate from nothing.
- **The lock step: right in kind, a term too large.** I took 6.2 us from one right half to the next; 470.81 - 465.01 = 5.80. The term that was mis-sized is the store, 0.37 us between squares and copies. ScalarE's row of the store starts with the squares, not behind them, and costs nothing. [rows 4] had misled me: there the root stands 0.38 us behind the store, but its bracket says that it waited for VectorE's mean. VectorE's waits ahead of the roots were 0.90 and twice 0.62 us, not 1.1 to 1.4 (timeline of ScalarE, after):

```profile
466.46 1.06 ACT L1342 ACTIVATE region_b<-region_a 128x1024 f32<-128x1024 f32 x1 [6.26 <-DVE region_a L1970]
466.48 0.33 ACTq L1353 DMA_DIRECT2D h_rows<-region_b  x1
...
467.52 1.06 ACT L1363 ACTIVATE region_b<-ps 128x512 f32<-128x512 f32 x2
468.48 0.20 ACT L1347 ACTIVATE sums<-sums 128x1 f32<-128x1 f32 x1
```

  Twice 0.4 us brings the samples' right half, with the clock up, to 59.28 us behind w_o's start (e6; I had 60.0), the logits of tile 2 to 481.8 (482.5) and the last logit 1.2 us earlier than before (0.5 forecast).
- **The fall of the clock: right, and it is most of the loss; the size was met by luck.** Over the 20 runs of after the time falls by 0.47 us for each 0.001 of mean clock (correlation -0.75). The mean clock over the runs is 0.982 for after and 0.988 to 0.989 for before (beside e1 to e8), 0.006 to 0.007 apart. By after's slope that is 2.8 to 3.3 us; by the slopes of before's own runs (0.32 to 0.37 us for 0.001) it is 1.9 to 2.6. The ratio says 3.0. Correlation alone would prove little; e8 and e12, e4 and e10 changed the waits and moved clock and time with them, and e6, which did it in after itself, went the same way without leaving after's interval.
  The +3.6 us booked are already the sum: 4.0 for the fall less 0.4 for the schedule. Measured are 874.75 - 871.70 = 3.05. The forecast of 874.8 fits to 0.1 us because the shift was 0.55 too large and the 871.22 it was put on, the median of 3 runs, 0.48 too low; and the 3.6 was the middle of a range from 1.0 to 6.2.
  Of the schedule's gain little arrives. At equal clock (0.987) lines fitted through the runs give 872.1 us for after and 871.3 to 872.2 for before. The traces show one place where it goes: in e6 the last logit comes 1.2 us earlier than in before, but the counting only 0.15, 77.71 us behind w_o's start for 77.86. The five products ahead of it end 1.1 us behind the one-hot rows (494.04), where I had them 0.4 ahead.
- **Where it falls: half right.** I had it between 480 and 496, behind a wait of 4.0 us. That place shows in e2 (2.89 us), e4 (3.37) and e8 (3.94), not in after's profiled execution. I gave the wait ahead of the logits of tile 0 (1.7 us forecast, 1.93 measured) no fall, and in after one came behind it; it cost 8 matmuls 0.20 us each and shortened the later wait to 1.48. My criterion "logits of tile 3 over 3 us" failed in after (1.96) and held in e3 and e8.
- **Rival 1 (no fall)** was never seen whole: 2 of after's 20 runs had a mean clock of 0.987, at 871.13 and 872.88 us, both above the 870.8 that I gave it.
- **Rival 2 (TensorE stays the bound)** named its condition, 4.9 us a tile, and its price, 865.8 to 868.5 us. e3, e7, e9 and e11 meet the condition (4.93 or 4.94 us from tile 2's right half to tile 3's), and in the last three, where the clock is held until about the last logits, the ratios are 0.9949 to 0.9969, which on before's 871.70 is 867.3 to 869.0 us. It was wrong for this kernel and right as a map to the better one.
- **Rival 3 (GpSimd's copies) is out.** The longest pair of copies takes 1.8 us of a block's 3.3, and TensorE's rows show no wait for GpSimd in the first pass. The first pair in the timeline of GpSimd of after:

```profile
402.30 1.03 POOL L1524 CAST cT<-hT_hi 128x8 fp32r<-128x8 f32 x1 [12.79 <-DVE hT_lo L1609]
403.28 0.18 POOL L1525 CAST cT<-hT_lo 128x8 fp32r<-128x8 f32 x1
```

  I had feared that they hold VectorE. It is the other way: VectorE's lo part of that moment ran its normal 1.22 us (402.06 to 403.28), and the copy of 8 columns, 0.18 alone, took 1.03 and ended with it. The Trainium skill (SBUF — State Buffer, section on the two separate sides) says of this port pair that one engine holds it for a whole instruction; the trace agrees.

## What to carry to other kernels

Work taken from TensorE can turn into waiting. Here waits of 1.5 to 3.9 us among short matmuls cost, through the granted clock, as much as the saved work or more. So read the clock of the stretch and place filler that is due anyway (here one gap product) into the wait. An order in which a tile's own root, squares and norm follow each other is a lock step of three engines; one tile of distance took 3.6 us out of it here. A gain at one mark may be gone at the next: compare the counting and the gather too, not only the last logit. And compare mean clocks over all runs, since one trace shows only one of the ways in which the clock can fall.

## What had not been expected of the hardware

- The same order up to that point, with waits of 0.53 and 0.55 us, had a fall of the clock at about 471.5 in e12 and none in e6. What decides it in an execution is open.
- A wait is not needed. In e6 the rows of TensorE show none between 481.76 and 489, only logits of 20 columns and transposes with a few wide matmuls between, and the clock fell at about 489.0. Around the last logits it fell, or was still down (e3, e8), in every profiled kernel but before. One unread matmul ahead of the samples' logits (e6, e7, e10, e11, e12) didn't prevent it.
- How long the clock stays down differs widely: 3.4 us twice in after, 13.6 in e3, 20.5 in e8. At the lower level a samples' matmul took 0.43 us for 0.23, a factor 1.86, and the logits 3.6 for 1.96; the prediction had 1.78 from [rows 6].
- The fall near 38 us [rows 5] lasts 13.6 us in before and about 3.4 in e3, e5 and e7. Those are the three traces in which w_o starts earliest (414.33 to 415.26 us, for 415.82 to 417.64 in the others). Part of the scatter between runs thus has nothing to do with the change, and the mean clock of a run mixes this fall with those of the stage: e3's profiled execution has 0.986, near before's 0.988, though its clock was down for 13.6 us in the stage.
